# Three changes to a three-block model kernel: four places for expert rows, zeroing moved, conditioning matrix shared by two engines

## The chip, the core and the metric

The kernel runs on one NeuronCore of a Trainium2 chip, in float32. The metric is the device time of one execution in microseconds (us). A core has TensorE (PE, matmuls; PEld is its weight load), VectorE (DVE), ScalarE (ACT), GpSimd (POOL) and SyncE (SP, which issues transfers here), 16 DMA engines, an on-chip memory of 128 partitions (SBUF) and PSUM, 8 banks of 512 floats on each partition, into which matmuls accumulate.

## What is computed

512 tokens of width 1024 pass three blocks in a row. Only two places of the reference matter here. The first block makes six rows of 1024 numbers out of one vector `c`:

```python
c_act = jax.nn.silu(c)                    # [1, 1024]
mod = c_act @ w_ada[l] + b_ada[l]         # w_ada is [1024, 6144], 25.2 MB
shift1, scale1, gate1, shift2, scale2, gate2 = jnp.split(mod, N_MOD, axis=-1)
h = modulate(rms_norm(x, norm1_g[l]), shift1, scale1)   # h * (1 + scale) + shift
```

The second block ends with a mixture of 16 experts, of which each token takes 2:

```python
h = jax.nn.silu(jnp.einsum('td,edf->tef', t, w_gate)) * jnp.einsum('td,edf->tef', t, w_up)
y = jnp.einsum('tef,efd->td', h * combine[..., None], w_down)   # d 1024, f 256
```

## The kernel before

The program is a chain of stages (`stage`, L42). Each ends with a barrier of all engines, so a stage starts when the slowest engine of the one before is through its instructions; transfers that nobody waited for may still be under way. Weights of ordinary projections come in pieces of 1 MB through `ring_raw`; `load_ahead` (L86) issues them from SP two pieces ahead. A weight is split into a high and a low part, and a product is three matmuls (`product`, L148 to L152).

**Conditioning stage** (`adaptive_rows`, L496). `w_ada` is cut into 12 chunks of 512 columns, each in two pieces of 1 MB: on each of 128 partitions four runs of 512 floats (2 KB). SP issues the 24 pieces into a ring of four slots (L510) and waits for `used` from the fifth on. TensorE multiplies each chunk in 8 plain fp32 matmuls of 128x512 (L536), with the activated `c` repeated over 128 columns as weights (`c_rep`), so that all 128 partitions get the same row. VectorE adds each chunk from PSUM to `mod`, into which the bias was loaded as 128 copies (L516, L551), and last applies the two norm gains (L555). ScalarE's queue issues the loads of the bias, of the two gains after chunk 3 and of `x` after chunk 6. Behind SP's 24 pieces stand two of `load_ahead`. The next stage is the norm (L422), whose VectorE work begins with L399.

**Start of the second block.** `build` (L2586) opens a stage `later_start`, in which SP issues 23 copies of 512 KB of zeros, DRAM to DRAM, into `moe_entries` (L2633), and GpSimd fills a few constants (L2637 to L2644). GpSimd waits for those copies only much later, in `moe`, before it scatters tokens. The next stage is the second block's first norm: its SP loads two rows, `row_a` and `row_b` (L445), and its VectorE waits for both before L467.

**Unit rows** (`unit_rows`, L1233) scales queries and keys of the delta branch: squares on ScalarE (L1250), sums and spreading on TensorE, the multiplication on VectorE. SP issues nothing in it.

**Sorted experts** (`moe`, L1965). Tokens are sorted by expert into 23 tiles of 128 rows (`ROW_TILES`) in DRAM; a tile belongs to one expert. For each tile s, SP loads 512 KB of rows (`enter`, L2029), TensorE turns them by 8 transposes (`turn_rows`, L2053), ScalarE and VectorE split the result (L2119, L2161), TensorE multiplies by gate and up (24 matmuls), ScalarE applies silu (L2131), VectorE multiplies (L2178), TensorE turns the hidden tile (L2078) and multiplies by the down weights (12 matmuls), ScalarE and VectorE evacuate one half each (L2139, L2167), and SP stores 512 KB (`leave`, L2033). The expert's weights come in three pieces of 1 MB a tile, gathered by GpSimd (L2011) into five places, a line of 8 KB on each partition, and are cut into high and low by ScalarE (L2112) and VectorE (L2155), in order, with four places for the cut pieces. TensorE's order in step s is: gate and up of s, turning of rows s+2, down of s-1, turning of the hidden tile s. SP's order is written out:

```python
enter(0)
enter(1)
for s in range(ROW_TILES):
    if s + 2 < ROW_TILES:
        enter(s + 2)      # waits until tile s is turned: two places
    if s:
        leave(s - 1)      # waits until tile s - 1 is evacuated
leave(ROW_TILES - 1)
```

## Time and profile before

| | before |
|---|---|
| median of 3 runs | 5193.03 us (5190.36 to 5204.13) |
| profiled execution | 5197.13 us, its span 5195.4 us |
| TensorE busy | 4090.6 us, 79% |
| VectorE busy | 3046.1 us, 59% |
| ScalarE, GpSimd busy | 17%, 19% |
| mean granted TensorE clock | 0.892 of full speed |
| read from and written to HBM | 859.00 and 30.41 MB |

The profile is of one execution. Busy time is the time in which an engine has an instruction of its kind running. In a row of the order of time stand the start and the duration in us, the engine and the line of the code, what is written and read, and in brackets how long the engine stood idle before and what released it. PEq, DVEq and the like are sequencers; a release by "PEq L49" or "PEq L45" is the end of a stage. A `MATMUL` in plain fp32 gives two records. The granted clock (PEclk) is 1.00 at 2.4 GHz and 0.50 at 1.2 GHz. The DMA share is the mean busy share of the 16 DMA engines.

### The profile page before, as it was taken

How to read it: one execution, taken by the hardware profiler on the slowest of the kernel's cores; microseconds unless marked ns; L12 is line 12 of the kernel's file. 1: busy time of each engine (PE TensorE's matmuls, PEld its weight loads, DVE VectorE, ACT ScalarE, POOL GpSimd, SP SyncE). 2: the span in 40 equal slices, each digit the busy share in tenths (PEclk: the TensorE clock that was granted, in tenths of full speed). 3: DMA queues.
4: the chain of work that ended last, by engine and by line, in shares of the span. 5: the costliest groups of instructions: out<-in, count | busy, mean ns of one | idle time of the engine just before them, and what ended most of it. 6: DMA issues, size and time to landing. Idle time of an engine off the chain costs nothing. (4 is left out here: it accounts for less than half of the span.)

```text
span 5195.4 us, 43884 instructions
## 1 busy us (share of the span) xinstructions
PE 4090.6 (79%) x15038; PEld 2713.0 (52%) x15038; DVE 3046.1 (59%) x5291; ACT 883.7 (17%) x1817; POOL 962.8 (19%) x841
## 2 busy tenths in 40 slices
PE   7889889778787777387879957857748887887987
PEld 3668666222222222155756734645536566676876
DVE  2343457778787786464546458536655346345774
ACT  0110011111111111011013134105531101311000
POOL 0000012344444443200002024024430000001001
PEclk9899889999999999787988977978878699598998
DMA  7212226999999999610120210227742022022221
GB/s 258 83 55 96 75 73 252 423 424 423 423 414 421 418 412 418 255 61 1 34 67 1 83 33 1 66 98 294 287 180 74 21 73 74 1 85 70 93 85 71
DMA packets 206449, 880.03 MB, mean 169 GB/s; under 512 B 21728, under 2 KB 24049, under 8 KB 131249
## 3 DMA queue, kind: packets, MB, share of 16 engines
q0 software_dynamic: 85968, 617.65, 29.1%
q1 hardware_dynamic: 119168, 253.47, 14.8%
q10 hardware_dynamic: 1104, 6.30, 0.3%
q8 instruction: 111, 1.82, 0.1%
q14 instruction: 98, 0.80, 0.0%
HBM read 859.00 MB, written 30.41 MB: 171 GB/s over the span
## 5 line engine op out<-in xcount | busy, mean ns | idle before, releaser
L122 DVE CAST ring_high<-ring_raw 128x2048 fp32r<-128x2048 f32 (+3 forms) x186 | 212.2, 1141 | 829.9 <-PE psum L152 759.6
L150 PE MATMUL psum<-ring_high,h_features 128*128 128x512 f32 x1120 | 445.5, 398 | 60.8 <-DVE ring_low L124 43.6
L906 PE MATMUL psum<-slots_ring,evacuation_tmp 128*128 128x512 f32 x816 | 403.6, 618 | 103.9 <-DVE evacuation_tmp L1004 103.6
L151 PE MATMUL psum<-ring_low,h_features 128*128 128x512 f32 x1120 | 443.5, 396 | 0.0
L152 PE MATMUL psum<-ring_high,h_features 128*128 128x512 f32 x1120 | 442.8, 395 | 0.0
L417 POOL TENSOR_SCALAR mean_var<-mean_var 128x1 f32<-128x1 f32 (+3 forms) x43 | 10.3, 239 | 2252.3 <-DVEq L1200 1041.4
L124 DVE TENSOR_TENSOR ring_low<-ring_raw,ring_high 128x2048 fp32r<-128x2048 f32 (+3 forms) x186 | 394.8, 2122 | 14.6 <-issue 0.4
L150 PE MATMUL psum<-h_features,ring_high 128*128 128x512 f32 (+4 forms) x920 | 365.2, 397 | 35.2 <-DVE ring_low L124 17.6
L151 PE MATMUL psum<-h_features,ring_high 128*128 128x512 f32 (+4 forms) x920 | 363.4, 395 | 0.0
L906 PE MATMUL psum<-slots_features,evacuation_tmp 128*128 128x512 f32 x612 | 301.9, 617 | 77.1 <-DVE evacuation_tmp L1004 77.1
L152 PE MATMUL psum<-h_features,ring_low 128*128 128x512 f32 (+4 forms) x920 | 362.5, 394 | 0.0
L906 PEld LDWEIGHTS psum<-slots_ring,evacuation_tmp 128*128 128x128 f32 x816 | 138.5, 189 | 367.9 <-DVE evacuation_tmp L1004 267.2
L1036 DVE CUSTOM_DVE_ANT_0 slots_ring<-slots_ring,h_tokens 128x1024 f32<-128x1024 f32 x204 | 249.7, 1224 | 102.0 <-DMA slots_ring<-in_peer_uv,expert 98.5
L1077 ACT ACTIVATE weight<-score 128x1 f32<-128x1 f32 x512 | 103.9, 203 | 1132.8 <-DVE score L1036 1132.7
L150 PEld LDWEIGHTS psum<-ring_high,h_features 128*128 128x128 f32 x1120 | 214.9, 192 | 110.3 <-issue 46.1
L853 POOL DMA_INDIRECT slots_ring<-in_peer_uv,expert x204 | 209.1, 1025 | 322.4 <-PE psum L906 290.6
L906 PE MATMUL psum<-slots_mod,evacuation_tmp 128*128 128x512 f32 x416 | 208.2, 625 | 56.5 <-DVE evacuation_tmp L1004 56.4
L906 PEld LDWEIGHTS psum<-slots_features,evacuation_tmp 128*128 128x128 f32 x612 | 104.1, 189 | 273.8 <-DVE evacuation_tmp L1004 198.6
L152 PEld LDWEIGHTS psum<-ring_high,h_features 128*128 128x128 f32 x1120 | 214.9, 192 | 45.9
L151 PEld LDWEIGHTS psum<-ring_low,h_features 128*128 128x128 f32 x1120 | 215.1, 192 | 44.8
L1036 DVE CUSTOM_DVE_ANT_0 slots_features<-slots_features,h_tokens 128x1024 f32<-128x1024 f32 x153 | 187.3, 1224 | 73.5 <-DMA slots_features<-in_peer_uv,expert 70.6
L150 PEld LDWEIGHTS psum<-h_features,ring_high 128*128 128x128 f32 (+4 forms) x920 | 169.1, 184 | 82.9 <-issue 28.0
(523 smaller groups left out, 7706.5 us busy)
## 6 DMA issues: line engine op xcount, KB each, us to landing
ring_raw<-in_w_in SPq DMA_DIRECT2D x94, 1024.0 KB, 5.2
ada_ring<-in_w_ada SPq DMA_DIRECT2D x24, 1024.0 KB, 5.7
ring_raw<-in_w_up_pairs SPq DMA_DIRECT2D x20, 1024.0 KB, 5.0
ring_raw<-in_w_out SPq DMA_DIRECT2D x12, 1024.0 KB, 5.0
moe_entries<-in_const_zero_rows SPq DMA_DIRECT2D x23, 512.0 KB, 15.8
row_room<-moe_entries SPq DMA_DIRECT2D x23, 512.0 KB, 8.9
moe_results<-row_room SPq DMA_DIRECT2D x23, 512.0 KB, 2.9
ring_raw<-in_w_down SPq DMA_DIRECT2D x10, 1024.0 KB, 4.9
```

Source lines behind the costliest of these rows:

```text
L122: nc.vector.tensor_copy(high, whole)
L124: return nc.vector.tensor_tensor(low, whole, high.bitcast(F32), ALU.subtract)
L150: nc.tensor.matmul(out, a[0], b[0], start=start, stop=False)
L151: nc.tensor.matmul(out, a[0], b[1], start=False, stop=False)
L152: return nc.tensor.matmul(out, a[1], b[0], start=False, stop=stop)
L417: nc.gpsimd.tensor_scalar(v, v, eps, None, ALU.add).then_inc(done, 1)
L853: nc.gpsimd.indirect_dma_start(out=slots[slot_of[n]], out_offset=None, in_=rows, in_offset=bass.IndirectOffsetOnAxis(ap=expert[:, t, i:i + ...
L906: mm = nc.tensor.matmul(banks(t)[q], diagonal[:, n % DIAGONALS, :], slots[slot_of[n]][:, D + q * BANK:D + (q + 1) * BANK], start=i == 0, s ...
L1036: nc.vector.tensor_tensor_reduce(out=u, in0=u, in1=core.h[:, t, :], scale=1.0, scalar=0.0, op0=ALU.mult, op1=ALU.add, accum_out=score[:, i ...
L1077: nc.scalar.activation(weight[:, i:i + 1], score[:, i:i + 1], ACT.Gelu).then_inc(activated, 1)
```

## The change

Three edits. **(1)** On the host `w_ada` is laid out as 6 rows x 4 quarters, so that a piece of 1 MB has one run of 2048 floats (8 KB) on each partition. The six rows are made in the order 1, 4, 0, 2, 3, 5. Of each row VectorE multiplies and adds the first three quarters (six steps of 128x1024, with the activated `c` as the scalar of each partition) into `sums`; TensorE takes the bias (a matmul with one row of ones), the last quarter (4 matmuls) and `sums` (2 matmuls with a matrix of ones, which adds up the partitions). The ring has eight places of 1 MB: the space of `h_features` and that of `ring_high` and `ring_low`. VectorE takes the two rows with a gain out of PSUM, ScalarE the other four. The bias is loaded once, 24 KB, instead of as 128 copies, and gains and `x` are issued when the first row is summed. **(2)** The 23 copies of zeros go from `later_start` to the stage of `unit_rows`. **(3)** The tiles of rows have four places (`ROWS_IN`), two of them a new buffer `more_rows`, and SP enters tile s+4 where it entered s+2.

```diff
+ADA_ORDER = (1, 4, 0, 2, 3, 5)
+ADA_PIECES, ADA_SUMMED = 4, 3
...
+    gains = {1: norm1_gain, 4: norm2_gain}
+    gained_at = {i: n for n, i in enumerate(i for i, r in enumerate(ADA_ORDER) if r in gains)}
+    in_features = over(nc, core.hT_whole, "ada_features", [P, ADA_PIECES, 2, D])
+    in_ring = over(nc, core.high, "ada_ring", [P, ADA_PIECES, 2, D])
+    ring = lambda i, q: (in_features, in_ring)[i % turns][:, q]
...
+        bank = lambda i: 2 * (i % 4)
+        landed_at = lambda i, q: (landed[ADA_PIECES * (i % turns) + q], 16 * (i // turns + 1))
...
         def _(sp):
-            for n, src in enumerate(pieces):
-                if n >= SLOTS:
-                    sp.wait_ge(used, n - SLOTS + 1)
-                sp.dma_start(ring[:, n % SLOTS, :].rearrange("p (k n) -> p k n", k=KD // 2), src).then_inc(landed[n % SLOTS], 16)
+            for i, r in enumerate(ADA_ORDER):
+                for q in range(ADA_PIECES):
+                    if i >= turns:
+                        if q < ADA_SUMMED:
+                            sp.wait_ge(used_summed, ADA_SUMMED * (i - turns) + q + 1)
+                        else:
+                            sp.wait_ge(used_direct, i - turns + 1)
+                    sp.dma_start(ring(i, q), d["w_ada_rows"][r, q].rearrange("p (k n) -> p k n", k=2)).then_inc(landed_at(i, q)[0], 16)
...
-            act.dma_start(mod[:].rearrange("p a f -> p (a f)"), d["b_ada"][0, :].partition_broadcast(P)).then_inc(bias_loaded, 16)
+            act.dma_start(bias[:], d["b_ada"]).then_inc(bias_loaded, 16)
...
-            act.wait_ge(multiplied, 3)
-            act.dma_start(norm1_gain, d["norm1_g"][0, :].partition_broadcast(P)).then_inc(rest_loaded, 16)
-            act.dma_start(norm2_gain, d["norm2_g"][0, :].partition_broadcast(P)).then_inc(rest_loaded, 16)
-            act.wait_ge(multiplied, 6)
-            act.dma_start(core.x[:], d["x"].rearrange("b (t p) f -> p (b t) f", p=P)).then_inc(rest_loaded, 16)
+            act.wait_ge(summed, 1)
+            act.dma_start(norm1_gain, d["norm1_g"][0, :].partition_broadcast(P)).then_inc(gains_loaded, 16)
+            act.dma_start(norm2_gain, d["norm2_g"][0, :].partition_broadcast(P)).then_inc(gains_loaded, 16)
+            act.dma_start(core.x[:], d["x"].rearrange("b (t p) f -> p (b t) f", p=P)).then_inc(x_loaded, 16)
+            for i, r in enumerate(ADA_ORDER):
+                if r not in gains:
+                    act.wait_ge(multiplied, i + 1)
+                    nc.scalar.copy(mod[:, r, :].rearrange("p (b n) -> p b n", b=2), core.ps[:, bank(i):bank(i) + 2, :]).then_inc(copied, 1)
+            act.wait_ge(x_loaded, 16)
 
         @block.tensor
...
-            for c, turn, odd, _ in pairs(pe, 0, chunks):
-                pe.wait_ge(evacuated, c + 1)
+            pe.wait_ge(bias_loaded, 16)
+            for i, r in enumerate(ADA_ORDER):
+                if i >= 4:
+                    pe.wait_ge(gained, gained_at[i - 4] + 1)
+                out = [core.ps[:, bank(i) + half, :] for half in range(2)]
+                cols = [slice(half * BANK, (half + 1) * BANK) for half in range(2)]
...
-                    slot = 2 * odd + half
-                    pe.wait_ge(landed[slot], 16 * (turn + 1))
-                    w = ring[:, slot, :].rearrange("p (k n) -> p k n", k=KD // 2)
-                    for k in range(KD // 2):
-                        kk = half * KD // 2 + k
-                        mm = nc.tensor.matmul(core.ps[:, odd, :], c_rep[:, kk, :], w[:, k, :], start=kk == 0, stop=kk == KD - 1)
-                    mm.then_inc(used, 1)
-                    if half == 1:
-                        pe.drain().then_inc(multiplied, 1)
+                    nc.tensor.matmul(out[half], ones[0:1, :], bias[:, r * D + half * BANK:r * D + (half + 1) * BANK], start=True, stop=False)
+                pe.wait_ge(*landed_at(i, ADA_SUMMED))
+                for k in range(2):
+                    for half in range(2):
+                        mm = nc.tensor.matmul(out[half], c_rep[:, k, :], ring(i, ADA_SUMMED)[:, k, cols[half]], start=False, stop=False)
+                mm.then_inc(used_direct, 1)
+                pe.wait_ge(summed, i + 1)
+                for half in range(2):
+                    mm = nc.tensor.matmul(out[half], ones[:], sums[:, i % 2, cols[half]], start=False, stop=True)
+                mm.then_inc(multiplied, 1)
...
-            dve.sem_inc(evacuated, 2)
+            def gain(i):
+                r = ADA_ORDER[i]
+                dve.wait_ge(gains_loaded, 32)
+                dve.wait_ge(multiplied, i + 1)
+                nc.vector.scalar_tensor_tensor(mod[:, r, :].rearrange("p (b n) -> p b n", b=2), core.ps[:, bank(i):bank(i) + 2, :], 1.0,
+                                               gains[r].rearrange("p (b n) -> p b n", b=2), ALU.add, ALU.mult).then_inc(gained, 1)
...
-            nc.vector.tensor_copy(c_rep[:], c_silu[:].unsqueeze(2).to_broadcast([P, KD, P])).then_inc(c_ready, 1)
-            dve.wait_ge(bias_loaded, 16)
...
-                dve.wait_ge(multiplied, j + 1)
-                part = rows[:, bass.ds(j * BANK, BANK)]
-                nc.vector.tensor_tensor(part, part, core.ps[:, odd, :], ALU.add).then_inc(evacuated, 1)
-            dve.drain()
...
+            nc.vector.tensor_copy(c_rep[:], c_silu[:, 2 * ADA_SUMMED:KD].unsqueeze(2).to_broadcast([P, 2, P])).then_inc(c_ready, 1)
+            for i, r in enumerate(ADA_ORDER):
+                if i >= 2:
+                    dve.wait_ge(multiplied, i - 1)
+                total = sums[:, i % 2, :]
+                for q in range(ADA_SUMMED):
+                    dve.wait_ge(*landed_at(i, q))
+                    for k in range(2):
+                        c = c_silu[:, 2 * q + k:2 * q + k + 1]
+                        if q + k == 0:
+                            done = nc.vector.tensor_scalar(total, ring(i, q)[:, k, :], c, None, ALU.mult)
+                        else:
+                            dve.drain()
+                            done = nc.vector.scalar_tensor_tensor(total, ring(i, q)[:, k, :], c, total, ALU.mult, ALU.add)
+                    done.then_inc(used_summed, 1)
+                    if q == 0 and i - 1 in gained_at:
+                        gain(i - 1)
+                dve.drain().then_inc(summed, 1)
...
+        @block.sync
+        def _(sp):
+            for s in range(ROW_TILES):
+                sp.dma_start(core.moe_entries[s * P:(s + 1) * P, :], d["const_zero_rows"]).then_inc(core.entries_cleared, 16)
...
-            rows_in, rows_out = room[:, 0:2, :], room[:, 2:4, :]
+            rows_in = lambda s: (room, more_rows)[s % ROWS_IN // 2][:, s % 2, :]
+            rows_out = room[:, 2:4, :]
...
                 def enter(s):
-                    if s >= 2:
-                        sp.wait_ge(row_turned, s - 1)
-                    sp.dma_start(rows_in[:, s % 2, :], tile(entries, s)).then_inc(row_in[s % 2], 16)
+                    if s >= ROWS_IN:
+                        sp.wait_ge(row_turned, s - ROWS_IN + 1)
+                    sp.dma_start(rows_in(s), tile(entries, s)).then_inc(row_in[s % ROWS_IN], 16)
...
-                enter(0)
-                enter(1)
+                for s in range(ROWS_IN):
+                    enter(s)
                 for s in range(ROW_TILES):
-                    if s + 2 < ROW_TILES:
-                        enter(s + 2)
+                    if s + ROWS_IN < ROW_TILES:
+                        enter(s + ROWS_IN)
                     if s:
                         leave(s - 1)
                 leave(ROW_TILES - 1)
...
-                        mm = nc.tensor.transpose(core.ps[:, bank_x[f // 4], f % 4 * P:(f % 4 + 1) * P], rows_in[:, s % 2, f * P:(f + 1) * P], core.ident[:])
+                        mm = nc.tensor.transpose(core.ps[:, bank_x[f // 4], f % 4 * P:(f % 4 + 1) * P], rows_in(s)[:, f * P:(f + 1) * P], core.ident[:])
...
-            @block.sync
-            def _(sp):
-                for s in range(ROW_TILES):
-                    sp.dma_start(core.moe_entries[s * P:(s + 1) * P, :], d["const_zero_rows"]).then_inc(core.entries_cleared, 16)
...
+    a["w_ada_rows"] = np.ascontiguousarray(a.pop("w_ada")[0].reshape(KD // 2, 2, P, 6, D).transpose(3, 0, 2, 1, 4)).reshape(6, KD // 2, P, 2 * D)
```

The order of instructions shows the first and the third edit. SP in the sorted experts before, from its first load of a tile of rows on (`row_room` holds the places, `moe_entries` the sorted rows in DRAM, `moe_results` the stored tiles; a store waits for its tile's evacuation):

```order
L2029 DMA row_room_20893<-moe_entries 128x1024 x4
L2033 DMA moe_results<-row_room_20893 128x1024
L2029 DMA row_room_20893<-moe_entries 128x1024
L2033 DMA moe_results<-row_room_20893 128x1024
L2029 DMA row_room_20893<-moe_entries 128x1024
```

The same place with the change (`more_rows` is the new buffer, places 3 and 4):

```order
L2079 DMA row_room_20990<-moe_entries 128x1024 x2
L2079 DMA more_rows<-moe_entries 128x1024 x2
L2079 DMA row_room_20990<-moe_entries 128x1024 x2
L2083 DMA moe_results<-row_room_20990 128x1024
L2079 DMA more_rows<-moe_entries 128x1024
L2083 DMA moe_results<-row_room_20990 128x1024
```

Four loads stood ahead of the first store, and six do now; the load behind the store of tile s-1 was that of tile s+3 and is that of tile s+5.

TensorE from the program's start, before (`ada_ring` holds the pieces of `w_ada`; the rows up to the branch are the body of a loop over pairs of chunks):

```order
L532 ISA
L536 MATMUL psum<-ada_ring_83,c_rep 128x512 x8
L529 REGISTER_ALU
L536 MATMUL psum<-ada_ring_83,c_rep 128x512 x8
L170 REGISTER_ALU
L170 COMPARE_AND_BRANCH
```

And with the change, the first two of six rows (`ada_features` and `ada_ring` are the two halves of the ring):

```order
L560 MATMUL psum<-bias,ones 128x512 x2
L564 MATMUL psum<-ada_features_83,c_rep 128x512 x4
L568 MATMUL psum<-sums,ones 128x512 x2
L560 MATMUL psum<-bias,ones 128x512 x2
L564 MATMUL psum<-ada_ring_84,c_rep 128x512 x4
L568 MATMUL psum<-sums,ones 128x512 x2
```

VectorE in the same two rows of the change:

```order
L591 TENSOR_SCALAR sums<-ada_features_83,c_silu 128x1024
L594 SCALAR_TENSOR_TENSOR sums<-ada_features_83,c_silu,sums 128x1024 x5
L591 TENSOR_SCALAR sums<-ada_ring_84,c_silu 128x1024
L594 SCALAR_TENSOR_TENSOR sums<-ada_ring_84,c_silu,sums 128x1024
L577 SCALAR_TENSOR_TENSOR mod<-psum,row_a 128x1024
L594 SCALAR_TENSOR_TENSOR sums<-ada_ring_84,c_silu,sums 128x1024 x4
```

The 96 matmuls with `c_rep` become 24, beside 12 on the bias and 12 on `sums`, and VectorE, which only added the results, now has six steps a row.

## Rows read from the trace of the kernel before

**Rows 1.** Windows: busy us of PE PEld DVE ACT POOL, PEclk, DMA share, GB/s

```profile
20.00:100.00 80.00, 74.13 (x165) 30.55 (x163) 6.96 (x11) 0.00 (x0) 0.00 (x0) 0.99 0.95 330
...
900.00:920.00 20.00, 15.95 (x33) 5.50 (x33) 15.75 (x35) 4.42 (x12) 7.95 (x9) 1.00 1.01 423
...
3500.00:3820.00 320.00, 235.14 (x968) 178.23 (x968) 205.87 (x173) 169.91 (x173) 134.82 (x64) 0.86 0.79 291
```

**Rows 2.** Waits of PE, 3515 to 3840 us: us in total, times, longest

```profile
PE psum L2053 <- DMA row_room<-moe_entries: 65.6, 12, 10.6
```

**Rows 3.** Waits of the SP queue, 0 to 130 us: total, times, longest

```profile
SPq L510 <- PE psum L536: 79.7, 20, 8.9
```

**Rows 4.** Order of time, conditioning stage: start us, us, engine line op [idle before]

```profile
7.61 5.84 PE L536 MATMUL psum<-ada_ring,c_rep 128*128 128x512 f32 x8 [7.61 <-DMA ada_ring<-in_w_ada]
...
84.73 7.11 PE L536 MATMUL psum<-ada_ring,c_rep 128*128 128x512 f32 x16 [0.36 <-issue]
...
107.37 0.69 DVE L551 TENSOR_TENSOR mod<-mod,psum 128x512 f32 x1 [6.78 <-PEq L539]
...
108.16 1.22 DVE L555 SCALAR_TENSOR_TENSOR mod<-mod,row_a 128x1024 f32<-128x1024 f32 x1
...
111.28 1.29 DVE L399 BATCH_NORM_STATS2 bn_parts<-x_tokens 128x6 f32<-128x512 f32 x2 [0.76 <-PEq L49]
```

**Rows 5.** Groups by line, 3500 to 3850 us: xcount, busy us, mean ns

```profile
L2189 DVE TENSOR_SCALAR x_tokens<-x_tokens 128x4096 f32<-128x4096 f32 x1 | 2.4, 2382 | 0.0
...
L2139 ACT COPY row_room<-psum 128x512 f32<-128x512 f32 x22 | 13.1, 597 | 12.7 <-PE psum L152 12.7
```

**Rows 6.** Order of time, sorted experts, engines PE and ACT

```profile
3521.04 0.38 ACT L2131 ACTIVATE silu_g<-psum 128x256 f32<-128x256 f32 x1 [3.06 <-PE psum L152]
...
3579.43 1.97 PE L2053 MATMUL psum<-ident,row_room 128*128 128x128 f32 x8 [5.45 <-DMA row_room<-moe_entries]
...
3591.58 1.09 PE L2053 MATMUL psum<-ident,row_room 128*128 128x128 f32 x8 [0.36 <-DMA row_room<-moe_entries]
...
3591.25 0.38 ACT L2131 ACTIVATE silu_g<-psum 128x256 f32<-128x256 f32 x1 [1.16 <-PE psum L152]
...
3601.99 0.38 ACT L2131 ACTIVATE silu_g<-psum 128x256 f32<-128x256 f32 x1 [1.10 <-PE psum L152]
...
3620.96 0.38 ACT L2131 ACTIVATE silu_g<-psum 128x256 f32<-128x256 f32 x1 [1.10 <-PE psum L152]
...
3836.21 0.38 ACT L2131 ACTIVATE silu_g<-psum 128x256 f32<-128x256 f32 x1 [5.47 <-PE psum L152]
```

**Rows 7.** Issues of the DMA view: xcount, KB each, median us to landing

```profile
ring_raw<-in_w_out SPq DMA_DIRECT2D x12, 1024.0 KB, 5.0
...
keysT<-in_sub_keys_t SPq DMA_DIRECT2D x1, 1024.0 KB, 4.9
...
row_room<-moe_entries SPq DMA_DIRECT2D x23, 512.0 KB, 8.9
```

**Rows 8.** Order of time, start of the second block

```profile
2159.95 14.63 SPq L2633 DMA_DIRECT2D moe_entries<-in_const_zero_rows  x23
...
2161.63 0.10 POOL L2644 MEMSET tile_row<- 128x4 f32 x1
...
2175.68 1.29 DVE L399 BATCH_NORM_STATS2 bn_parts<-x_tokens 128x6 f32<-128x512 f32 x2 [16.58 <-PEq L49]
...
2176.03 0.66 SPq L445 DMA_DIRECT2D row_b<-in_ln_b  x1
...
2203.63 1.23 DVE L467 TENSOR_TENSOR h_tokens<-h_tokens,row_a 128x1024 f32<-128x1024 f32 x1 [22.29 <-DMA row_b<-in_ln_b]
```

**Rows 9.** Order of time around the stage of the unit rows

```profile
2312.17 4.26 ACT L1250 ACTIVATE squares<-qkvT 128x512 f32<-128x512 f32 x8 [3.43 <-PEq L49]
...
2341.79 0.47 DVE L1129 TENSOR_SCALAR g_row<-g_row,dt_bias 4x512 f32<-4x512 f32 x1 [0.75 <-PEq L49]
...
2545.08 0.35 SPq L209 DMA_DIRECT2D gain<-in_gdn_norm  x1
```

More of the change, by code:

```diff
@@ L493, with _ @@
 SGU_GROUPS, SGU_DIM = 4, 256
+ADA_ORDER = (1, 4, 0, 2, 3, 5)
+ADA_PIECES, ADA_SUMMED = 4, 3
 def adaptive_rows(nc, core, d, mod, norm1_gain, norm2_gain):
-    chunks = 6 * D // BANK
-    pieces = [half for j in range(chunks) for half in kmajor(d["w_ada"][0], j * BANK, BANK)]
-    ring = over(nc, core.hT_whole, "ada_ring", [P, SLOTS, PIECE])
-    with buffers(nc, c_col=[P, KD], c_silu=[P, KD], c_rep=[P, KD, P]) as (c_col, c_silu, c_rep), \
-            stage(nc, "ada", "c_loaded", "bias_loaded", "rest_loaded", "silu_done", "c_ready", "multiplied", "used", "evacuated",
-                  *[f"landed{n}" for n in range(SLOTS)]) as (
-                block, c_loaded, bias_loaded, rest_loaded, silu_done, c_ready, multiplied, used, evacuated, *landed):
+    turns = 2
+    gains = {1: norm1_gain, 4: norm2_gain}
[3 more added lines that the diff above has]
+    ring = lambda i, q: (in_features, in_ring)[i % turns][:, q]
+    with buffers(nc, c_col=[P, KD], c_silu=[P, KD], c_rep=[P, 2, P], ones=[P, P], sums=[P, 2, D], bias=[1, 6 * D]) as (
+            c_col, c_silu, c_rep, ones, sums, bias), \
+            stage(nc, "ada", "c_loaded", "bias_loaded", "gains_loaded", "x_loaded", "ones_ready", "silu_done", "c_ready", "used_summed", "used_direct",
+                  "summed", "multiplied", "copied", "gained", *[f"landed{n}" for n in range(turns * ADA_PIECES)]) as (
+                block, c_loaded, bias_loaded, gains_loaded, x_loaded, ones_ready, silu_done, c_ready, used_summed, used_direct,
+                summed, multiplied, copied, gained, *landed):
+        bank = lambda i: 2 * (i % 4)
+        landed_at = lambda i, q: (landed[ADA_PIECES * (i % turns) + q], 16 * (i // turns + 1))
+        @block.gpsimd
+        def _(pool):
+            nc.gpsimd.memset(ones[:], 1.0).then_inc(ones_ready, 1)
@@ L552, in _ @@
-            dve.drain()
-            dve.wait_ge(rest_loaded, 48)
-            for which, gain in ((1, norm1_gain), (4, norm2_gain)):
-                nc.vector.scalar_tensor_tensor(mod[:, which, :], mod[:, which, :], 1.0, gain, ALU.add, ALU.mult)
+            def gain(i):
[4 more added lines that the diff above has]
+                                               gains[r].rearrange("p (b n) -> p b n", b=2), ALU.add, ALU.mult).then_inc(gained, 1)
```

21 lines of the change are left out of this document (10 added, 11 removed).

## The prediction

> **What bounds the kernel now.** The windows come first [rows 1]: three stretches with the busy time of each engine, the granted clock, the busy share of the 16 DMA engines and their GB/s. Between 20 and 100 us (the conditioning stage) TensorE is busy 74.1 of 80 us at 0.99 of its full clock while the DMA engines are busy 0.95 of the time at 330 GB/s: both are near their end. The window at 900 us lies in the gather of the first block's experts, where lines of 8 KB arrive at 423 GB/s and share 1.01. In the sorted experts (3500 to 3820 us) nothing is full: TensorE 235 of 320 us, VectorE 206, ScalarE 170, DMA share 0.79. So the next view is the waits of that stretch [rows 2]: TensorE stands 65.6 us in 12 waits for a tile of sorted rows to come back from DRAM. The third place, the zeroing ahead of the second block, is read from the order of time below. I cost each apart.
>
> **Conditioning matrix.** Before, SP waited 79.7 us for TensorE to free ring slots [rows 3], so TensorE sets the pace and DMA is close behind. It runs twelve chunks of 8 fp32 matmuls; a chunk's 16 records (two a matmul) take 7.11 us [rows 4], so 0.89 us a matmul. The stage ends where the next norm's first VectorE work starts, at 111.3 us [rows 4].
> After, TensorE has 8 matmuls for each of six rows (2 bias, 4 on the fourth quarter, 2 on VectorE's sums): 8 x 0.89 = 7.1 us a row. VectorE has per row one multiply and five multiply-adds of 128x1024. A scalar_tensor_tensor of that size took 1.22 us, and 0.10 us passed over the drain before it [rows 4]; a tensor_scalar from SBUF 2.38 us for 4096 columns, so 0.6 us for 1024 [rows 5]; a row is 0.6 + 5 x 1.32 = 7.2 us (7.8 if the multiply runs no faster than the other), plus 1.3 us for the two rows with a gain. Both are less than what the DMA needs. Its bytes: 24 pieces of 1.05 MB are 25.2 MB, the two gains 1.05, x 2.1, together 28.3 MB; the bias broadcast of 3.1 MB falls to 24 KB.
> The rate is the unknown. Upper bound 423 GB/s, the gather's lines of 8 KB [rows 1]. Lower bound the present stage, 330 GB/s at share 0.95, so 347 at full share, from lines of 2 KB. I take 423, since the lines will be 8 KB: 28.3 / 0.423 = 66.9 us. Before, the first piece was used at 7.6 us [rows 4]; less its own 2.5 us of transfer the stream begins near 5.1, and the last piece lands at 72.0. Then 4 + 2 matmuls (5.3 us), some of them at the low clock: TensorE will have waited some 4 us a row, and after such a wait 8 transposes took 1.97 us instead of 1.09 [rows 6], so I add 1.7. One ScalarE copy of 1024 columns is twice 0.6 us [rows 5], the barrier 0.8: the norm starts at 81.0 us. **Gain 30.3 us.** At 347 GB/s the last piece lands at 86.7 and the gain is 15.6.
> One early stall costs nothing: VectorE's first gain waits for a load that ScalarE only issues after row 0 is summed, so perhaps 6 us, but eight pieces are out by then and the queue stays full.
> A row that speaks against the wide lines: alone on the queue, a 1 MB load of 2 KB lines takes 5.0 us from issue to landing and one of 8 KB lines 4.9 [rows 7]. The Trainium skill (DMA: Bandwidth & Descriptors, Specifications) says that lines of 512 B or more reach line rate. By that rule 8 KB lines gain nothing over 2 KB; the trace leaves it open, 423 against 347 being two kinds of transfer. The same page (Where 436 GB/s comes from) says that some 358 GB/s from HBM bind a core; by it this load would take 79 us. The 423 GB/s read from HBM here contradict it.
>
> **Zeroing moved.** Before, 23 copies of 512 KB hold SP for 14.63 us while GpSimd is done at 2161.7. The next norm starts at 2175.7, 1.1 us behind SP's last issue, then VectorE waits 22.3 us for the norm's second row, which queues behind the zeros and is only there at 2203.6 [rows 8]. After, the norm starts 1.1 us behind GpSimd, at 2162.8: 12.9 us. The wait of 22.3 us goes too: VectorE comes to it 5.7 us after the norm's start, and a transfer twice as large landed 4.9 us after issue [rows 7], the row being issued 0.4 us in; I leave 0.3. **Gain 34.9 us**, bounds 31 to 35.2.
> The same 23 copies then stand in the stage of the unit rows, which lasts from 2312.2 to 2341.8 us [rows 9]: 29.6 us of ScalarE, TensorE and VectorE work in SBUF and PSUM cover 14.6 us of SP. The transfers took 2160 to 2204, so 44 us; moved, they end some 15 us after that stage, and the next transfer that SP issues is at 2545 [rows 9]. Nothing queues behind them. Cost 0; without that cover it would be the 14.6 us again.
>
> **Four places for rows.** Tile s+3's load is issued behind the store of tile s-1, which waits for both evacuations; TensorE wants it one gate-and-up later. It takes 8.9 us to land in the median [rows 7], and at 3579.4 TensorE had stood 5.45 us for one [rows 6]. With four places the load behind that store is tile s+5's: two tiles more of lead, over 20 us against 8.9. So the 65.6 us end, and the slow matmuls after each wait with them.
> What is late next? From ScalarE's first silu (3521.0) to the 23rd (3836.2) are 22 steps, 14.33 us each; a step without a wait took 3602.0 - 3591.3 = 10.7 us [rows 6], and that is TensorE's own pace. A tile moves three pieces, a tile of rows in and one out, 4.19 MB. The stretch ran 291 GB/s at share 0.79, so 368 at full share: 11.4 us a tile if the engines never pause. VectorE is busy 206/320 of 14.33, so 9.2 us, ScalarE 7.6. DMA takes over as the bound. I take 11.6 us, near that: (14.33 - 11.6) x 22 = **60 us**. Upper bound TensorE's 10.7 us, 80 us gained (DMA at 4.19/10.7 = 392 GB/s, under the gather's 423). Lower bound 33 us, half of the waiting coming back as waits for pieces, since ScalarE and VectorE cut them in order.
>
> **Sum.** 30.3 + 34.9 + 60 = 125.2 us from the profiled execution's 5197.1 us gives 5071.9. That execution is 4.1 us above the median of the runs, 5193.0, so I predict **5068 us**.
>
> **The rivals.**
> A. The lines do not matter: the conditioning stage stays at 347 GB/s. For it the two landing times [rows 7] and the rule above, against it the 423 [rows 1]. 5193.0 - 15.6 - 34.9 - 60 = 5082.5 us.
> B. Pieces replace rows: the DMA engines are shared by two queues, and ScalarE's in-order cuts wait for pieces where TensorE waited for rows. For it the share of 0.79 already; against it that no wait for a piece stands in the present loop. 5193.0 - 30.3 - 34.9 - 33 = 5095 us.
> C. The change does not do what it says: rows stay late, because loads and stores still share SP's one queue and a load stands behind a store that waits. Against it the lead counted above. 5193.0 - 65.2 = 5128 us.
> D. Slower than before. Four row loads ahead take their share from the pieces, and a piece late at ScalarE holds its silu and evacuation too, so that each tile takes what only every other takes now, 3621.0 - 3602.0 = 19.0 us [rows 6]. That is 4.6 x 22 = 102 us lost against 65.2 gained: 5230 us. It decides from 18.0 us a tile, which is 233 GB/s, where the stretch has 291; so it is unlikely.
>
> **How the numbers follow.** Forecast 0.67, A 0.12, B 0.12, C 0.05, D 0.03, and 0.01 that the parts just cancel. Fast end: 33 + 35 + 80 = 148 us gained, 5045. Slow end: A and B together, 15.6 + 31 + 33, about 80 us gained, 5113. I give 5043 to 5115, which leaves out C, D and little else. A measurement of this kernel tells 0.3%, 15.6 us, from no change; all cases but D and the last are beyond it: faster 0.96, same 0.01, slower 0.03.
>
> **What would show it.** The first norm's statistics start near 81 us, with 400 GB/s or more between 20 and 60 us; 95 us and 350 GB/s would be A. The second block's norm runs with no wait for its rows, and the stage of the unit rows keeps its 29.6 us. In the experts TensorE's waits for rows vanish but for the first tile, silu follows silu every 11 to 12 us evenly, and the DMA share passes 0.9. Waits of ScalarE or TensorE for pieces of 1.5 us a tile or more would be B. I am wrong if the three gains do not add, or if the tile's step stays over 13 us.

## The result

| | before | with the change |
|---|---|---|
| median of 4 runs, in turn on the same chip | 5196.61 us (5190.36 to 5204.13) | 5043.85 us (5041.51 to 5048.59) |
| profiled execution, span | 5197.13, 5195.4 us | 5045.18, 5043.5 us |
| ratio of the times | | 0.9705, 95% interval 0.9692 to 0.9719 |

The change saves 152.8 us, 2.9%. The forecast was 5068 us in a range of 5043 to 5115. Two of the three parts gave what was forecast; the third, the rows, gave more, and the time lies at the fast edge of the range, 0.85 us inside it.

SyncE loads some small tensors in every stage. The time between two such loads splits both profiles at the same places of the program:

| stretch | before | after | difference |
|---|---|---|---|
| start to the load of `final_g` (conditioning stage, first block) | 2144.6 | 2113.9 | -30.7 |
| to `gdn_conv_c` (start of the second block, its norm) | 78.0 | 42.6 | -35.4 |
| `router_bias` to `in_ln_g` (sorted experts) | 441.6 | 359.6 | -82.0 |
| `gla_w` to `gla_norm` (nothing in it was edited) | 209.5 | 202.3 | -7.2 |
| everything else | 2321.7 | 2325.1 | +3.4 |

The page of the changed kernel, first its engines, then its two large DMA queues (packets, MB, share of 16 engines):

```profile
PE 4025.7 (80%) x14942; PEld 2673.8 (53%) x14942; DVE 3076.8 (61%) x5315; ACT 885.9 (18%) x1821; POOL 965.8 (19%) x842
...
q0 software_dynamic: 85968, 617.65, 29.9%
q1 hardware_dynamic: 109952, 253.47, 14.7%
```

TensorE has 64.9 us less work and VectorE 30.7 us more than before, and nearly all bytes are the same ones. Zeroing and rows save waiting and no work; only in the conditioning stage did work go from one engine to another.

The windows of the changed kernel (busy us of PE, PEld, DVE, ACT, POOL, then PEclk, DMA share, GB/s), three from the conditioning stage and one from the sorted experts, answer to [rows 1]:

```profile
5.00:20.00 15.00, 8.41 (x10) 3.24 (x11) 9.42 (x9) 0.21 (x1) 0.00 (x0) 1.00 1.01 425
20.00:40.00 20.00, 14.80 (x27) 5.29 (x26) 10.96 (x10) 0.00 (x0) 0.00 (x0) 0.91 1.01 417
40.00:60.00 20.00, 16.96 (x32) 6.77 (x32) 14.83 (x13) 2.02 (x2) 0.00 (x0) 0.83 1.02 422
...
3460.00:3640.00 180.00, 166.99 (x762) 124.92 (x762) 157.97 (x137) 127.80 (x131) 109.25 (x52) 1.00 0.99 385
```

The conditioning stage now runs at 417 to 425 GB/s up to 60 us (411 from 60 to 75 us) where it ran at 330. In the experts TensorE is busy 93% of the time (73% before) at the full clock (0.86 before), and the DMA engines are at 385 GB/s where they were at 291.

The end of the conditioning stage in order of time, to be held against [rows 4]:

```profile
62.93 6.71 PE L564 MATMUL psum<-ada_features,c_rep 128*128 128x512 f32 x8 [2.59 <-DMA ada_features<-in_w_ada_rows]
65.46 0.75 DVE L591 TENSOR_SCALAR sums<-ada_ring,c_silu 128x1024 f32<-128x1024 f32 x1 [2.06 <-DMA ada_ring<-in_w_ada_rows]
66.29 1.28 DVE L594 SCALAR_TENSOR_TENSOR sums<-ada_ring,c_silu,sums 128x1024 f32<-128x1024 f32 x1
67.94 5.38 DVE L594 SCALAR_TENSOR_TENSOR sums<-ada_ring,c_silu,sums 128x1024 f32<-128x1024 f32 x4 [0.36 <-DMA ada_ring<-in_w_ada_rows]
...
73.20 3.70 PE L564 MATMUL psum<-ada_ring,c_rep 128*128 128x512 f32 x8
76.74 1.88 PE L568 MATMUL psum<-sums,ones 128*128 128x512 f32 x4
78.65 1.01 ACT L546 COPY mod<-psum 128x1024 f32<-128x1024 f32 x1 [6.24 <-PE psum L568]
80.51 1.29 DVE L398 BATCH_NORM_STATS2 bn_parts<-x_tokens 128x6 f32<-128x512 f32 x2 [7.19 <-PEq L48]
```

The norm starts at 80.51 us (111.28 before). Both engines wait for pieces in the fifth and sixth row, so the transfers set the pace. The same four matmuls (8 records) took 6.71 us behind a wait and 3.70 us in the sixth row, which TensorE came to without a wait: the granted clock in the windows above is a mixture of its two levels, down to 0.83 in the rows shown.

The start of the second block, to be held against [rows 8], and the zeroing where it stands now, to be held against [rows 9]:

```profile
2130.87 0.10 POOL L2689 MEMSET tile_row<- 128x4 f32 x1
...
2131.72 1.29 DVE L398 BATCH_NORM_STATS2 bn_parts<-x_tokens 128x6 f32<-128x512 f32 x2 [3.25 <-PEq L48]
...
2137.57 1.25 DVE L466 TENSOR_TENSOR h_tokens<-h_tokens,row_a 128x1024 f32<-128x1024 f32 x1 [0.19 <-issue]
...
2246.36 15.07 SPq L1285 DMA_DIRECT2D moe_entries<-in_const_zero_rows  x23
2246.38 4.26 ACT L1298 ACTIVATE squares<-qkvT 128x512 f32<-128x512 f32 x8 [3.42 <-PEq L48]
...
2275.99 0.47 DVE L1172 TENSOR_SCALAR g_row<-g_row,dt_bias 4x512 f32<-4x512 f32 x1 [0.75 <-PEq L48]
```

The norm starts 0.75 us behind the end of GpSimd's last memset, and VectorE's wait of 22.29 us for `row_b` is gone. The stage of the unit rows lasts from 2246.38 to 2275.99, 29.6 us, as before.

The sorted experts: ScalarE's silus in order of time, to be held against [rows 6]; the first three, then two neighbours from the even part, then the last:

```profile
3448.55 0.38 ACT L2181 ACTIVATE silu_g<-psum 128x256 f32<-128x256 f32 x1 [2.94 <-PE psum L151]
3456.01 0.39 ACT L2181 ACTIVATE silu_g<-psum 128x256 f32<-128x256 f32 x1 [0.43 <-PE psum L151]
3468.00 0.38 ACT L2181 ACTIVATE silu_g<-psum 128x256 f32<-128x256 f32 x1 [1.12 <-PE psum L151]
...
3564.99 0.39 ACT L2181 ACTIVATE silu_g<-psum 128x256 f32<-128x256 f32 x1 [1.12 <-PE psum L151]
3575.77 0.38 ACT L2181 ACTIVATE silu_g<-psum 128x256 f32<-128x256 f32 x1 [1.14 <-PE psum L151]
...
3682.67 0.38 ACT L2181 ACTIVATE silu_g<-psum 128x256 f32<-128x256 f32 x1 [5.50 <-PE psum L151]
```

22 steps in 3682.67 - 3448.55 = 234.1 us are 10.64 us each (14.33 before). The mean takes in a short first and last step (7.5 and 9.9 us); those between are even, about 10.8 us, where before about every other one took 17 to 23 us and the rest 10.7. And in the waits from 3400 to 3740 us TensorE's only one for rows (answering to [rows 2]) is that for the first tile:

```profile
PE psum L2103 <- DMA row_room<-moe_entries: 30.8, 1, 30.8
```

### The profile page after: what moved, and what is told of

Its sections match the earlier page's. It is cut to its first block and busy times, and to the rows that moved or that the text cites. A ratio compares the mean times of both kernels' runs of the same rounds, so it can differ in the third digit from the quotient of the medians.

```text
span 5043.5 us, 43677 instructions
## 1 busy us (share of the span) xinstructions
PE 4025.7 (80%) x14942; PEld 2673.8 (53%) x14942; DVE 3076.8 (61%) x5315; ACT 885.9 (18%) x1821; POOL 965.8 (19%) x842
## 5 line engine op out<-in xcount | busy, mean ns | idle before, releaser
L151 PE MATMUL psum<-ring_high,h_features 128*128 128x512 f32 x1120 | 441.6, 394 | 0.0
L149 PE MATMUL psum<-h_features,ring_high 128*128 128x512 f32 (+4 forms) x920 | 365.6, 397 | 35.7 <-DVE ring_low L123 18.1
L151 PE MATMUL psum<-h_features,ring_low 128*128 128x512 f32 (+4 forms) x920 | 362.8, 394 | 0.0
```

What stands on the lines that cost most here:

```text
L149: nc.tensor.matmul(out, a[0], b[0], start=start, stop=False)
L151: return nc.tensor.matmul(out, a[1], b[0], start=False, stop=stop)
```

## The experiments

The first nine of them (e1 to e9) ran beside the kernel before on the same chip. A ratio is that of the times to the kernel before, with its 95% interval. "Stats" is the start of the first norm's statistics.

**The three parts alone (e1, e2, e3).** Each of these kernels is the kernel before with one of the three edits. The first takes over the change's `moe`:

```diff
-RAW_PIECES, CUT_PIECES = 5, 4
+RAW_PIECES, CUT_PIECES, ROWS_IN = 5, 4, 4
...
-                    if s >= 2:
-                        sp.wait_ge(row_turned, s - 1)
+                    if s >= ROWS_IN:
+                        sp.wait_ge(row_turned, s - ROWS_IN + 1)
```

> The kernel before with the four places for rows alone. Theory (the parts add, and the sorted experts now run at TensorE's own step): silu to silu 10.6 to 10.8 us against 14.33 before, 22 steps, so 79 to 83 us less than before, about 5115 us. Rival (part of those 81 us comes from the other two edits, for instance a warmer start or zeros that landed earlier): 60 us or less.

The second moves the 23 copies from the start of the second block to `unit_rows`:

```diff
+        @block.sync
+        def _(sp):
+            for s in range(ROW_TILES):
+                sp.dma_start(core.moe_entries[s * P:(s + 1) * P, :], d["const_zero_rows"]).then_inc(core.entries_cleared, 16)
...
-            @block.sync
-            def _(sp):
-                for s in range(ROW_TILES):
-                    sp.dma_start(core.moe_entries[s * P:(s + 1) * P, :], d["const_zero_rows"]).then_inc(core.entries_cleared, 16)
```

> The kernel before with the zeroing moved alone. Theory: 12.9 us of issuing and 22.3 us of waiting for the norm's rows go and nothing comes back, 35 us less than before, about 5161 us. Rival (the transfers slow something behind the unit rows): 20 us or less.

The third takes over the change's `adaptive_rows` and its ordering of `w_ada`:

```diff
-                sp.dma_start(ring[:, n % SLOTS, :].rearrange("p (k n) -> p k n", k=KD // 2), src).then_inc(landed[n % SLOTS], 16)
+                    sp.dma_start(ring(i, q), d["w_ada_rows"][r, q].rearrange("p (k n) -> p k n", k=2)).then_inc(landed_at(i, q)[0], 16)
```

> The kernel before with the conditioning stage of the change alone. Theory: the first norm starts at 80.5 us instead of 111.3, 31 us less than before, about 5166 us. Rival (what the stage gains is given back at the first projection, whose pieces are now issued behind a fuller queue): under 20 us.

| | median us | ratio | gain us | its own stretch |
|---|---|---|---|---|
| before | 5195.98 | | | |
| rows alone (e1) | 5115.66 | 0.9848 [0.9832, 0.9864] | 80.3 | silu step 10.64 us |
| zeroing alone (e2) | 5158.27 | 0.993 [0.9913, 0.9946] | 37.7 | `final_g` to `gdn_conv_c` 42.7 us (78.0) |
| conditioning alone (e3) | 5165.14 | 0.9946 [0.9928, 0.9964] | 30.8 | stats at 81.95 us (111.28) |

The three gains sum to 148.8 us, against 152.8 for all together: the parts add, within what the intervals allow. Two of them have the size of their term (34.9 and 30.3 us). The rows' term was 60 us and they give 80.

**Are the lines or the shared sums what speeds the conditioning stage (e4, e5)?** The change with lines of 2 KB in place of 8 KB, all else kept:

```diff
-sp.dma_start(ring(i, q), d["w_ada_rows"][r, q].rearrange("p (k n) -> p k n", k=2)).then_inc(landed_at(i, q)[0], 16)
+sp.dma_start(ring(i, q).rearrange("p k (h n) -> p (k h) n", h=2), d["w_ada_rows"][r, q].rearrange("j p n -> p j n")).then_inc(landed_at(i, q)[0], 16)
```

> The changed kernel whose pieces of the conditioning matrix have four lines of 2 KB on each partition instead of one of 8 KB; who multiplies what is unchanged. Theory (2 KB lines reach 347 GB/s at full share, 8 KB lines 423): 28.3 MB take 81.6 us, the first norm starts near 95 us instead of 80.5, the kernel is 14 us slower than the change, about 5058 us. Rival (lines of 512 B or more all run at line rate): the norm starts at 80 to 82 us, the kernel is within 3 us of the change.

And the other way round: the kernel before, its 96 matmuls kept, with its pieces stored in lines of 8 KB:

```diff
-    pieces = [half for j in range(chunks) for half in kmajor(d["w_ada"][0], j * BANK, BANK)]
+    pieces = [d["w_ada_lines"][j, half].rearrange("p (k n) -> p k n", k=KD // 2) for j in range(chunks) for half in range(2)]
```

> The kernel before whose 24 pieces of the conditioning matrix are laid out as one line of 8 KB on each partition; TensorE still multiplies all of it, in 96 matmuls. Theory (TensorE set the pace of that stage, its chunks of 7.5 us are 12 x 7.5 = 90 us): the first norm starts at 107 to 111 us, 0 to 4 us gained, about 5193 us. Rival (the stage was held by its transfers, the shared work is not needed): the norm starts near 85 us, 25 us gained.

The change with 2 KB lines took 5059.77 us, ratio 0.9732 [0.9706, 0.9758]. Its norm's start and the windows of its conditioning stage:

```profile
88.54 1.29 DVE L398 BATCH_NORM_STATS2 bn_parts<-x_tokens 128x6 f32<-128x512 f32 x2 [10.11 <-PEq L48]
```

```profile
20.00:40.00 20.00, 10.29 (x19) 4.07 (x18) 9.47 (x8) 0.00 (x0) 0.00 (x0) 0.66 1.04 396
40.00:60.00 20.00, 17.11 (x32) 6.51 (x31) 14.30 (x12) 1.01 (x1) 0.00 (x0) 0.84 1.05 387
```

So the DMA engines are full here too, at 387 to 396 GB/s against 417 to 422 with lines of 8 KB, and the norm starts 8.0 us later, where I had expected 14. The kernel's time, 15.9 us over the change, looks like that expectation, but by chance: its four runs spread from 5040.86 to 5066.63 us, and of the 18.5 us between the two profiles 7.0 lie ahead of `final_g` and 11.4 in a stage far behind that no kernel here edits (e10).

The kernel before with 8 KB lines took 5189.33 us in 10 runs, ratio 0.9991 [0.9981, 1.0001]: no difference that can be measured. Its stats start at 108.94 us, 2.3 us earlier. The windows, and SP's wait for TensorE (us in total, times, longest; 79.7 in [rows 3]):

```profile
20.00:40.00 20.00, 18.55 (x42) 7.55 (x42) 2.06 (x3) 0.00 (x0) 0.00 (x0) 1.00 0.88 332
40.00:60.00 20.00, 18.21 (x42) 7.54 (x41) 2.06 (x3) 0.00 (x0) 0.00 (x0) 1.00 0.90 328
```

```profile
SPq L510 <- PE psum L536: 78.6, 20, 10.2
```

The wider lines lower the DMA share between 20 and 100 us (0.95 to 0.89) at nearly the same rate (330 and 334 GB/s), and TensorE paces it as before. Of the 30.8 us, 22.7 come from all that the change does there beside the lines (the change at 2 KB lines against before) and 8.0 from the lines; alone the lines are worth 2.3. The 22.7 are put down to the work taken off TensorE, since TensorE set the pace before; but the larger ring and the bias loaded once came with it, and no run separates the three. Rival A, by which the lines do not matter and the norm starts at about 95 us, falls: the lines do matter, and even with 2 KB the norm starts at 88.5.

**How many places do the rows need (e6)?** The change with three places:

```diff
-RAW_PIECES, CUT_PIECES, ROWS_IN = 5, 4, 4
+RAW_PIECES, CUT_PIECES, ROWS_IN = 5, 4, 3
...
-            rows_in = lambda s: (room, more_rows)[s % ROWS_IN // 2][:, s % 2, :]
+            rows_in = lambda s: (room[:, s % 3, :] if s % 3 < 2 else more_rows[:, 0, :])
```

> The changed kernel with three places for the tiles of rows instead of four. The load behind the store of tile s-1 is then that of tile s+4: one tile of lead, some 10.7 us more than before the change. Theory (a row takes 9 to 12 us to land, the lead is 4 us plus 10.7): no waits for rows beyond the first, steps of 10.6 to 10.8 us, the time of the change within 3 us, 5044 us. Rival (with fuller DMA queues a row takes over 15 us and the fourth place is needed): waits for rows of 2 us or more a tile, 40 us slower than the change.

5043.45 us, ratio 0.9707 [0.9691, 0.9723], the same as with four. The silus run from 3462.00 to 3694.45, a step of 10.57 us, and beyond the first tile TensorE waits for rows once, 0.9 us in all. One place more than before is enough; the fourth buys nothing that can be measured.

**What paces the experts now, TensorE or the DMA engines (e7, e8)?** TensorE gets less to do and the same bytes flow: in the gate and up products the low half of the rows times the high half of the weights is left out.

```diff
-                            mm = product(nc, core.ps[:, bank_g[s % 2], :], [rowT(part, s)[:, kk, :] for part in range(2)],
-                                         [v[:, k, :] for v in w], kk == 0, kk == KD - 1)
+                            nc.tensor.matmul(core.ps[:, bank_g[s % 2], :], rowT(0, s)[:, kk, :], w[0][:, k, :], start=kk == 0, stop=False)
+                            mm = nc.tensor.matmul(core.ps[:, bank_g[s % 2], :], rowT(0, s)[:, kk, :], w[1][:, k, :], start=False, stop=kk == KD - 1)
```

> The changed kernel without one of the three matmuls of each product of gate and up in the sorted experts (low rows times high weights), so 8 matmuls of 0.23 us less for each of 23 tiles: that part of the computation is left out. Theory (TensorE sets the step of 10.64 us, the DMA engines have a little room above the 385 GB/s that they now move at share 0.99): the step falls to 10.0 to 10.4 us, where DMA at 400 to 420 GB/s holds it, 5 to 14 us faster than the change. First rival (the DMA engines are full at share 0.99 and already set the step): step 10.6 to 10.9 us, no change in time. Second rival (TensorE alone matters): step 8.8 us, 40 us faster.

And TensorE's work kept with more bytes: one copy of 512 KB from DRAM to DRAM a tile, to a scratch that nobody reads.

```diff
                     sp.dma_start(rows_in(s), tile(entries, s)).then_inc(row_in[s % ROWS_IN], 16)
+                    sp.dma_start(tile(core.moe_extra, s), d["const_zero_rows"]).then_inc(core.extra_done, 16)
```

> The changed kernel with one more transfer of 512 KB of zeros, DRAM to DRAM, issued behind each load of a tile of rows. 23 such copies took 44 us alone, so 1.9 us of all DMA engines a tile. Theory (4.19 MB a tile at up to 410 GB/s need 10.2 us of the step of 10.64, little room): the step becomes 10.2 + 1.9 = 12.1 us, 32 us slower than the change. Rival (the true capacity is the 368 GB/s that share and rate of the kernel before gave, and the step only stays short by prefetching): 11.4 + 1.9 = 13.3 us, 58 us slower. Second rival (much room left): step 10.7 us, under 5 us slower.

With less for TensorE: 5032.78 us, ratio 0.9692 [0.9675, 0.9709]. The first and the last silu, and the window of 180 us:

```profile
3443.38 0.39 ACT L2181 ACTIVATE silu_g<-psum 128x256 f32<-128x256 f32 x1 [0.92 <-PE psum L2118]
...
3659.38 0.38 ACT L2181 ACTIVATE silu_g<-psum 128x256 f32<-128x256 f32 x1 [3.07 <-PE psum L2118]
```

```profile
3460.00:3640.00 180.00, 151.14 (x684) 110.39 (x683) 165.16 (x144) 137.82 (x144) 86.39 (x54) 0.98 1.01 416
```

The step falls from 10.64 to 216.0 / 22 = 9.82 us, a little below the 10.0 to 10.4 that I had expected. The mean hides two paces: from the fifth to the nineteenth step it is 10.03 us (about 10.8 in the change), and the last three steps take 8.2 to 8.7. The same bytes now pass at 416 GB/s, and ScalarE waits for pieces (waits, 3400 to 3760 us), which it never does in the change from 3460 to 3640 us:

```profile
ACT ring_high L2162 <- DMA raw<-in_moe_rows,pieces_of: 21.8, 20, 2.3
...
ACT last_cut L2162 <- DMA raw<-in_moe_rows,pieces_of: 13.3, 12, 2.1
...
ACT third_cut L2162 <- DMA raw<-in_moe_rows,pieces_of: 9.6, 10, 1.8
```

So TensorE sets the 10.64 us of the change. The next bound is most likely the DMA engines, at about 416 GB/s; this run alone does not tell them from VectorE, which is busy 165 of 180 us and for whose `hidden` TensorE waits 27.2 us, in 20 waits. By the medians the kernel is only 11.1 us faster than the change, by the silus 18.1; its four runs spread over 17.5 us.

With more traffic: 5057.49 us, ratio 0.9733 [0.9716, 0.9749], but the silus tell how little of that lies in the experts:

```profile
3463.79 0.38 ACT L2182 ACTIVATE silu_g<-psum 128x256 f32<-128x256 f32 x1 [1.39 <-PE psum L151]
...
3703.60 0.38 ACT L2182 ACTIVATE silu_g<-psum 128x256 f32<-128x256 f32 x1 [5.48 <-PE psum L151]
```

```profile
3460.00:3640.00 180.00, 163.20 (x749) 121.99 (x748) 150.92 (x129) 124.66 (x129) 73.10 (x50) 1.00 1.01 422
```

The step is 239.8 / 22 = 10.90 us, 0.26 us more (in the middle 11.15 against 10.8), and the stretch of the experts 362.8 us against 359.6. The medians lie 13.6 us apart; in the profiles 11.4 us of the difference stand in the stage that nobody edited (e10). I had expected 12.1 us, by adding the copy to a queue that I took to be full. It was not: at share 0.99 and 385 GB/s there was room for another 37 GB/s, and the waits of ScalarE for pieces only begin there (28.4, 16.3 and 13.3 us in the three kinds of piece). VectorE is busy only 151 of 180 us here and the rate is again about 420 GB/s, so that rate, and not VectorE, is what the two kernels have in common: the bound by traffic is 416 to 422 GB/s.

**Does the place of the zeroing matter, or only that it is behind the norm's rows (e9)?** The change with its 23 copies issued in the second block's first norm, right behind that norm's two rows:

```diff
                 for buf, vec in rows:
                     sp.dma_start(buf, vec.partition_broadcast(P)).then_inc(rows_loaded, 16)
+                if name == "norm0_2":
+                    for s in range(ROW_TILES):
+                        sp.dma_start(core.moe_entries[s * P:(s + 1) * P, :], core.zero_rows).then_inc(core.entries_cleared, 16)
```

> The changed kernel with the 23 copies of zeros issued in the second block's first norm, behind its two rows, instead of in the stage of the unit rows. That norm lasts some 25 us, so the 14.6 us of issuing are covered there too. Theory (what stands behind the zeros in SP's queue pays: the taps, the level masks and the first weight pieces of the delta branch's projection, issued some 25 us later, land only when the 44 us of zeros are through): the projection starts its convolution some 15 to 20 us late, 12 to 20 us slower than the change. Rival (any covered place does, since transfers interleave): within 3 us of the change.

5050.89 us, ratio 0.9726 [0.9707, 0.9745]. The zeros do delay a load behind them, as the waits of the stretch behind the norm (2130 to 2240 us) say:

```profile
DVE ring_high L121 <- DMA ring_raw<-in_w_in: 18.5, 1, 18.5
```

But VectorE stood at that place in the change, too: there it waits 9.7 us for TensorE to free the ring, and 23.8 us in its four such waits of this window, where this kernel has 7.4 us of them beside the 18.5. The stretch with the norm comes out at 42.6 us, as in the change, and the next one (to `gdn_norm`), with the projection, at 323.9 against 323.0 and 321.3 us in two profiles of the change. So the collision costs 0.9 to 2.6 us and not the 12 to 20 that I had expected; the slack of the projection takes in the rest. What is won with the zeroing is won by letting the norm's rows go first and by freeing the barrier of SP; the cover of the unit rows stage is not what it needs. Whether the 7.0 us between the medians come from this edit is the next question.

**The stage that nobody edited (e10, e11).** The change and the kernel before, each in one more execution, with no edit (so there is no diff):

> The change once more, nothing edited. The stage between the loads of gla_w and gla_norm (second block, nothing in it edited) took 202.3 us in the change's first profile and 209.5 us in that of before, and in the experiments 202.4 (e3, e7), 209.5 (e1), 210.7 (e2, e5) and 213.8 us (e4, e6, e8, e9). Theory: this is variation of TensorE's granted clock from execution to execution, so the 7.2 us are no part of the edits' gain; then this run may show any of the levels, 202, 210 or 214 us, and 210 or more would show it. Rival: the level belongs to the program (its alignment in time before the stage); then 202.3 us within 0.5. The conditioning stage, the delta branch and the experts come out as in the first profile, within 1 us: 2113.9, 42.6 and 359.6 us between loads.

> The kernel before once more, nothing edited. Theory of variation: the stage from gla_w to gla_norm may come out at 202, 210 or 214 us; anything but 209.5 shows it. Rival (the level belongs to the program): 209.5 us within 0.5.

| | time us | start to `final_g` | to `gdn_conv_c` | experts | `gla_w` to `gla_norm` |
|---|---|---|---|---|---|
| change, first profile | 5045.18 | 2113.9 | 42.6 | 359.6 | 202.3 |
| change again | 5051.6 | 2112.5 | 42.6 | 358.3 | 213.8 |
| before, first profile | 5197.13 | 2144.6 | 78.0 | 441.6 | 209.5 |
| before again | 5192.97 | 2145.8 | 78.9 | 436.9 | 209.5 |

The windows of that stage, of the first profile of the change and of the second:

```profile
2579.44:2781.79 202.35, 167.00 (x732) 114.94 (x732) 109.80 (x147) 59.33 (x138) 42.60 (x33) 0.86 0.08 25
```

```profile
2577.86:2791.70 213.84, 176.82 (x732) 121.59 (x732) 106.81 (x147) 59.29 (x138) 42.07 (x33) 0.82 0.08 24
```

The same 732 matmul records take 9.8 us longer at a granted clock of 0.82 instead of 0.86. One and the same program shows 202.3 and 213.8 us, so the 7.2 us of the table at the top are no part of the gain that can be put down to an edit. That the time of this stage belongs to the program falls. Whether it goes with the execution or with the chip is open, since it is not known whether the two profiles of the change are of one chip; the two profiles of the kernel before agree (209.5 us), and say nothing on it. Nor is it shown what sets the clock here. The kernel with the zeros in the norm (e9) had 213.8 us there as well: its profiled execution of 5056.64 us is 11.5 us behind the first of the change, as is its stage. Against the second profile of the change, with the same 213.8, it is 5.0 us longer, of which 2.6 lie in the projection and 2.4 ahead of `final_g`, where its program is the same; so up to 2.6 us can be put down to its edit, and the 7.0 us between the medians cannot. The edited stretches come out within 1.4 us in the change; the experts of before vary by 4.7 us, so the rows' gain is known to about that: 77.3 to 83.3 us by these four profiles.

None of the kernels tried beats the change by more than the measurement can tell, but for the one that leaves out a part of the products.

## Why the prediction was right, and where its sizes were off

**Conditioning, 30.3 us forecast, 30.8 measured.** The norm starts at 80.51 us for 81.0. The rate was taken as 423 GB/s and is 411 to 425. VectorE's row was put at 7.2 us: its first step took 0.75 us for 0.6, and the four that follow one another 5.38 us, 1.34 each for 1.32, all hidden. The tail was right for a slightly other reason. The last four matmuls came at the full clock (3.70 us); it was the fifth row's four, at 6.71 us, that held the sixth row's bias matmuls up, so they started at 73.2 and not at 72.0. That 1.2 us late and 1.7 us not needed nearly cancel is luck. The early stall of VectorE (6 us estimated) was 8.3 us, and the queue stayed full through it: 417 GB/s between 20 and 40 us. The split inside the term was wrong, though. I let the lines carry the whole step from 347 to 423 GB/s, half of the gain; they carry 8.0 us.

The Trainium skill's rule (DMA: Bandwidth & Descriptors, Specifications) that lines of 512 B or more reach line rate is not what the runs show: 387 to 396 GB/s with 2 KB against 417 to 422 with 8 KB, both with full engines. With 2 KB lines the norm starts about midway between what that rule (80.5 us) and what my lower bound (95 us) would give. The 358 GB/s from HBM of the Trainium skill (DMA: Bandwidth & Descriptors, Where 436 GB/s comes from) is exceeded in every full window of the conditioning stage and of the experts here, 377 to 425 GB/s; the page works it out as half of what two cores share, and this program ran on one.

**Zeroing, 34.9 us forecast, 35.4 between the loads, 37.7 by the kernel with this part alone.** Each step stands: the norm starts 0.75 us behind GpSimd's end (1.1), the wait for the norm's second row is gone, the 23 copies hold SP for 15.07 us (14.6) under a stage that keeps its 29.6 us. What I named as the cover is more than is needed, by the experiment with the zeros in the norm.

**Rows, 60 us forecast, 77.3 to 83.3 measured.** What the edit does was right: the waits for rows vanish but for the first tile, and the lead is long enough (row loads now take 11.2 us to land in the median, and three places would do). The step that failed is what paces the loop next, and with it the size of the term; it is the one that reads "The stretch ran 291 GB/s at share 0.79, so 368 at full share: 11.4 us a tile ... DMA takes over as the bound. I take 11.6 us". TensorE's own pace is the bound, 10.64 us, which stood in the prediction as the upper bound of 80 us. A share of 0.79 at 291 GB/s doesn't mean 368 at 1.00: the same mix of transfers ran at 385 with share 0.99 and at 416 with share 1.01. The same division sized the lower bound of the conditioning stage, 330 at 0.95 "so 347 at full share", and it failed there in the same way, with 387 to 396 measured. With 22 steps of 14.33 - 10.64 us, 81 us, in place of 60, the forecast would have been 5047, against 5043.85; the 3 us left are less than what the clock of the stage nobody edited moves between two profiles of the change. That the time lies in the range at all is in part luck: the fast end was worked out as 148 us gained, 152.8 were measured, and 5043.85 clears 5043 by less than 1 us.

**The rivals.** A (the lines don't matter, 5082.5): the norm starts at 80.5, and even with 2 KB lines at 88.5, not at 95. B (pieces replace rows, 5095): in the change no wait for a piece between 3460 and 3640 us. They come at 9.82 us a tile or at 422 GB/s, beyond where the change stands. C (rows stay late, 5128): one wait left. D (19.0 us a tile, 5230): 10.64. (Its 4.6 x 22 is 101 and not 102 us, and the difference of the two steps is 4.67; that moves nothing.)

**The signs that were named.** Norm near 81 us with 400 GB/s or more: yes. Second block's norm without a wait: yes. Unit rows at 29.6 us: yes. Silus evenly every 11 to 12 us: evenly, but at 10.8 in the middle and 10.64 in the mean. DMA share past 0.9: yes, 0.99.

## What to carry to other kernels

Where an engine's waits are to be removed, look for a step of the loop in which the wait did not occur: it is the loop's pace with the waits gone, a better estimate here (10.7 for 10.64) than any sum over shares. A DMA share below 1 is no measure of the room that is left; the rate of a stretch in which the queues are really full is, and it has to be taken with lines of the same length and the same kinds of transfer. And a long transfer is cheap where it queues behind the small ones that somebody waits for, and dear where it queues ahead of them: the same 23 copies cost 35 us ahead of two rows and 1 to 3 us behind them.

## What the runs showed of the hardware that was not expected

- A share that says full has room: from 385 GB/s at 0.99 to 416 and 422 at 1.01. And full is not one rate: the 23 copies from DRAM to DRAM, nearly alone on the engines, run at 293 to 319 GB/s with shares of 0.92 to 1.01 (kernel before, 2170 to 2200 us). A 512 KB copy from DRAM to DRAM added to every tile made the tile 0.26 us longer (0.4 in the middle of the loop), where 23 of them on their own take 44 us, 1.9 each.
- With full engines, 128 lines of 8 KB run at 411 to 425 GB/s and 512 lines of 2 KB at 383 to 396 (377 in the kernel before between 60 and 75 us; its 413 between 5 and 20 us has the 128 copies of the bias among them), though alone on the queue loads with either length land in 4.9 to 5.0 us [rows 7]. Under a load that TensorE paces (332 GB/s) the longer lines only lower the share, from 0.95 to 0.89.
- TensorE's granted clock in a stage far behind every edit gives one program 202.3 us in one profile (mean clock 0.86) and 213.8 in another (0.82). Differences of 10 us between two profiles of this kernel have to be looked for by stage before they are put down to an edit.
